# Differential attention: score matmuls of the two maps taken in turn from the two halves of TensorE's rows

## The reference, cut to what matters

```
s = jnp.einsum("bhiqd,bhikd->bhiqk", q, k).astype(jnp.float32) * scale   # i = 0, 1: two maps, d = 64
p = jax.nn.softmax(sc, axis=-1)
a = (p[:, :, 0] - lam_full * p[:, :, 1]).astype(v.dtype)
return jnp.einsum("bhqk,bhkd->bhqd", a, v)
```

## Time and profile before

| | us |
|---|---|
| median of 3 runs | 5064.48 |
| lowest, highest | 5056.97, 5072.84 |
| span of the profiled execution | 5071.2 |
| layer 1's attention in it, from the first score matmul to the last output copy | 925.3 |
| TensorE busy in the span | 4675.7 |

### The profile page before, as it was taken

How to read it: one execution, slowest core, us unless ns; L and a number is a source line. 1 busy time by engine, 2 the same in 40 slices (tenths; PEclk the granted TensorE clock), 3 DMA queues, 4 the chain that set the end, 5 groups by cost and what they waited for, 6 DMA issues and landing times. The chain is left out here.

```text
span 5071.2 us, 72044 instructions
## 1 busy us (share of the span) xinstructions
PE 4675.7 (92%) x29100; PEld 3834.2 (76%) x29100; DVE 1472.4 (29%) x2638; ACT 1065.5 (21%) x2197; POOL 558.0 (11%) x551
## 2 busy tenths in 40 slices
PE   7799999999689999999958999999895999999995
PEld 2377777774479999999955666666655999999995
DVE  6533344442311111111145444444422111111113
ACT  4333333331001111111122333333210111111112
POOL 0210000002310000000032000000032000000002
PEclk9899999999789999999979999999997999999997
DMA  8650010010356676776640000000106777777774
GB/s 310 202 193 20 20 39 20 20 42 30 130 174 238 236 241 236 240 241 233 236 139 31 13 13 12 12 12 12 47 33 223 256 246 255 253 252 251 255 255 150
DMA packets 563237, 737.79 MB, mean 145 GB/s; under 512 B 33680, under 2 KB 420352, under 8 KB 563032
## 3 DMA queue, kind: packets, MB, share of 16 engines
q1 hardware_dynamic: 533112, 642.58, 37.7%
q0 software_dynamic: 22352, 67.94, 3.7%
q10 hardware_dynamic: 7704, 26.31, 1.3%
HBM read 675.65 MB, written 65.05 MB: 146 GB/s over the span
## 5 line engine op out<-in xcount | busy, mean ns | idle before, releaser
L1444 PE MATMUL ps<-item_xT,expert_ring 128*128 128x160 f32 (+1 forms) x10496 | 1369.5, 293 | 6.8 <-issue 2.4
L1444 PEld LDWEIGHTS ps<-item_xT,expert_ring 128*128 128x128 f32 x10496 | 1360.4, 191 | 18.0 <-issue 18.0
L1466 PE MATMUL ps<-item_aT,expert_ring 128*128 128x144 f32 (+1 forms) x5248 | 763.6, 302 | 0.0
L1466 PEld LDWEIGHTS ps<-item_aT,expert_ring 128*128 128x128 f32 x5248 | 724.2, 198 | 5.5
L277 PE MATMUL ps<-hT,w_group 128*128 128x512 f32 (+1 forms) x1408 | 535.2, 539 | 6.0 <-ACT df_probs L1077 3.9
L1505 DVE TENSOR_TENSOR item_aT<-item_silu,ps 128x144 f32<-128x144 f32 (+1 forms) x328 | 102.4, 312 | 1249.4 <-ACT item_silu L1480 1249.4
L277 PEld LDWEIGHTS ps<-hT,w_group 128*128 128x128 f32 x1408 | 266.9, 192 | 257.1 <-issue 244.8
L1480 ACT ACTIVATE item_silu<-ps 128x144 f32<-128x144 f32 (+1 forms) x328 | 97.3, 297 | 1158.1 <-PE ps L1444 1158.1
L385 PE MATMUL ps<-hT,oT 128*128 128x512 f32 x576 | 254.2, 602 | 16.8 <-DMA router_w<-in_router_w 16.8
L1512 DVE COPY item_y<-ps 16x512 f32<-16x512 f32 (+1 forms) x82 | 55.7, 679 | 736.3 <-PE ps L1457 736.3
L1483 ACT ACTIVATE item_yT<-ps 128x144 f32<-128x144 f32 (+1 forms) x328 | 97.2, 296 | 811.7 <-PE ps L1466 811.7
(11 more groups left out here) (186 smaller groups left out, 4626.9 us busy)
## 6 DMA issues: line engine op xcount, KB each, us to landing
expert_ring<-in_expert_w_gate SPq DMA_DIRECT2D x164, 1024.0 KB, 5.0
expert_ring<-in_expert_w_up SPq DMA_DIRECT2D x164, 1024.0 KB, 7.2
expert_ring<-in_expert_w_down SPq DMA_DIRECT2D x82, 2048.0 KB, 10.0
mod_ring<-in_mod_w SPq DMA_DIRECT2D x24, 2048.0 KB, 11.1
w_group<-in_w_qkv SPq DMA_DIRECT2D x48, 512.0 KB, 4.8
slot_out<-item_y ACTq DMA_DIRECT2D x41, 512.0 KB, 7.1
slot_out<-rows POOLq DMA_DIRECT2D x5, 4096.0 KB, 36.4
h_rows<-hr SPq DMA_DIRECT2D x18, 512.0 KB, 2.6
```

The source lines that it names most:

```text
L1444: m = nc.tensor.matmul(gub(b, w), ring[:, b // 2, k, w * 256 + (b % 2) * P:w * 256 + (b % 2 + 1) * P], xT[:, k, :], start=k == 0, stop=k = ...
L1466: m = nc.tensor.matmul(yb(j), ring[:, 4 + j // 4, f, (j % 4) * P:(j % 4 + 1) * P], aT[:, f, :], start=f == 0, stop=f == FB - 1)
```

## The change

The two functions for scores become one. It waits for both exponentials of the previous tile before its first matmul, and its matmuls go in the order map 0 columns 1024 to 1279, map 1 columns 256 to 767 (in its own count), map 0 columns 0 to 511, then after the wait on `s_half` map 1's 256 columns, map 0 columns 512 to 1023, and map 1's last 512. The first increment of `s_S` comes with the fifth matmul, the second with the sixth. Matmuls, their sizes, their banks and all other engines' streams stay as they are.

```diff
-                        def scores(t, m, which):
+                        def score(t, m, n):
                             r = slice(m * HD, (m + 1) * HD)
-                            for n in which:
-                                c0, k0, w = parts[m][n]
-                                mm = nc.tensor.matmul(ps[:, c0:c0 + w], qT[r, t * P:(t + 1) * P], kT[r, k0:k0 + w], start=True, stop=True)
-                            return mm
-
-                        def scores_first(t):
+                            c0, k0, w = parts[m][n]
+                            return nc.tensor.matmul(ps[:, c0:c0 + w], qT[r, t * P:(t + 1) * P], kT[r, k0:k0 + w], start=True, stop=True)
+
+                        def scores(t):
                             if t:
 
-                                pe.wait_ge(s_exp, g * 2 * LT + 2 * t - 1)
-                            scores(t, 0, (0,))
-
-                        def scores_rest(t):
-                            if t:
-
                                 pe.wait_ge(s_exp, g * 2 * LT + 2 * t)
-                            scores(t, 0, (2,)).then_inc(s_half, 1)
-                            scores(t, 0, (1,))
+                            score(t, 0, 2).then_inc(s_half, 1)
+                            score(t, 1, 1)
+                            score(t, 0, 0)
 
                             pe.wait_ge(s_half, g * LT + t + 1)
-                            scores(t, 1, (0,)).then_inc(s_S, 1)
-                            scores(t, 1, (1, 2)).then_inc(s_S, 1)
+                            score(t, 1, 0)
+                            score(t, 0, 1).then_inc(s_S, 1)
+                            score(t, 1, 2).then_inc(s_S, 1)
...
-                        scores_first(0)
-                        scores_rest(0)
+                        scores(0)
...
-                        scores_first(1)
-                        scores_rest(1)
+                        scores(1)
...
-                                scores_first(t + 2)
-                                scores_rest(t + 2)
+                                scores(t + 2)
```

## The result

The changed kernel takes 5089.42 us (median of 9 runs, 5082.37 to 5108.4) against 5064.48 us (9 runs, 5051.89 to 5079.66). The ratio is 1.006, 95% interval 1.0041 to 1.0078: slower by about 30 us by the ratio and by 25 between the medians, where 13 us less were forecast. The profiled execution took 5108.4 us, with a span of 5106.4. It is the slowest of the nine, so the profile shows more of the loss than the median holds. The granted clock over its span was 0.944, the lowest of the nine (up to 0.949), and 0.954 in the profiled execution before.

What follows compares the result with a forecast made beforehand. TensorE was taken to bound each group's start, the VectorE and ScalarE loop tiles 2 to 7. Terms -1.41, -0.02, -0.20, -0.03 and 0 gave -1.66 per group, -13.3 us for 8 groups: 5064.5 to 5051.2, range 5036 to 5074.

Steps and rivals of the forecast that it cites:

- The ring: Tiles 2 to 7: combine, normalise, maxima and exponentials on VectorE and ScalarE set the 8.43 us period, without a TensorE wait.
- Rival 3: All tiles: TensorE bounds every one, so 90 us go and the time is 4974; chance 0.03.
- The lanes: Score passes: two row halves stream side by side; scores to next load take 2.54 us, not 3.95, 1.41 less per tile.
- rivals 1 and 2: Score passes: first, starts follow program order, end 2.98, +2 us, chance 0.10; second, long matmuls do not overlap, +74 us, 0.08.
- The sum at the start of a group: Tiles 0 and 1: earlier scores and V projection, shorter maxima and exponential wait; -1.66 us per group.
- Nothing gained, nothing lost: Tiles 2 to 7: VectorE is free 2.46 us after the load, map 0 ready at 2.45, so no change.
- rival 4: Clock: half-clock stretches in layer 1's experts may fall otherwise, up to 35 us; no fall expected in attention; chance 0.09.
- the sign, a clock under 1.00 in the stage: Attention stage of the changed profile: a granted clock below full would mean rival 4.
- theory B: Put for the experiments, on the scores: using both halves of the rows at once brings TensorE's clock down.
- theory C: Put for the experiments, on the scores: the later wait does the harm by itself, whatever the order; +25 us or more.
- The margin of 0.01 us: Tiles 2 to 7: slack between map 0 ready and VectorE free; each 0.1 us later costs 4.8 us there.
- The head start given up: Tiles 2 to 7: 0.56 us of TensorE score work ahead of the exponential is lost, paid for by the 1.41 saved.

Runs made afterwards that it cites:

- the split maximum: Alternating kernel without the full wait, VectorE's normalise behind the next maxima, plus map 1's maximum taken in two parts, bank 2 first; 4999.26 us, ratio 0.9857.
- the small filler's run: Changed kernel plus one unread 128-column matmul per tile between the second and third products with V; 5057.26 us, ratio 0.9971.
- the start-only run: Kernel before, with the new order and wait in tiles 0 and 1 of each group alone; 5055.84 us, ratio 0.9975.
- the last version: The split maximum's kernel, with tile 0 of each group given the changed kernel's full alternation; 4995.09 us, ratio 0.9845 against the kernel before.

## Why the prediction was wrong

- **The ring as bound of tiles 2 to 7: right.** Tiles at full clock kept 8.43 with scores 1.6 us shorter; cutting 0.43 out of VectorE's part of the ring gave 8.01, and the split maximum up to 7.27. Rival 3, TensorE as bound, is out.
- **The lanes: right in kind, the term too large.** The scores with what follows take 2.35 (3107.47 to 3109.82, below), not 2.54. I let the second half's first weights wait for two loads of the first half. In the trace the first loads of the two halves start 6 ns apart. Two 512-wide passes do run together at full rate: rivals 1 and 2 are out. The Trainium skill (TensorE: Matmul & The Clock Gate, Part 3) states that matmuls start in program order, by which rival 1 came to 2.98; the 2.35 of the trace doesn't agree.

TensorE after, group 3, tile 0, which answers to the earlier trace rows:

```profile
3107.47 2.42 PE L957 MATMUL ps<-df_kT,df_qT 64*128 64x256 f32 x12
3109.82 0.38 PE L937 MATMUL ps<-w_group,hT 128*128 128x128 f32 x1
```

- **The sum at the start of a group: right, mis-sized.** -1.87 per group where -1.66 was put, by the shorter scores. Where the clock holds, the gain comes out: the small filler's run and the start-only run are 15 and 13 us faster than before.
- **"Nothing gained, nothing lost" in tiles 2 to 7, the failed step.** It stood on rival 4's sentence "I expect no fall there, as products or scores fill most of each ring". I had counted the idle time, 1.2 to 1.7 us in 8.43, and judged it harmless without a price, because the whole stage had shown a clock of 1.00. That row was taken with a nearly full TensorE and said nothing of the new state. The clock fell 30 times, 29 of them under scores, and each fall cost 1.66 us: +49.7 against -15.0. The prediction had named the sign, a clock under 1.00 in the stage. That less work on TensorE ahead of the scores brings the fall was shown by adding work to the change and by taking work from the old order; theory B was refuted by the alternation without the full wait, theory C by the wait without the alternation. What counts as work, beyond busy time, stays open.
- **The margin of 0.01 us** was named, and it is what made a fall so dear: scores at half clock come 1.7 us late on a ring with no slack for them. The head start given up, 0.56 us ahead of the exponential, would have taken up a part of that; no run measures this by itself.
- **The chances.** Slower had 0.11, most of it for a mechanism that did not occur. The clock had 0.09, split evenly over the three outcomes, though in the changed stage it could only go down.

The Trainium skill (TensorE: Matmul & The Clock Gate, Part 1: The HAM clock gate) describes a gate that lets through half the clock when TensorE has lately done too little. The trace agrees in kind: 1.67 of 3.42 us busy, then half clock. Its section on a second failure mode (psum-queue depth-cycling) names short idle stretches between groups of matmuls, again and again, as enough to make the clock swing; 30 falls at gaps of 1.1 to 1.2 and 0.5 to 0.6 us agree. I had the gaps computed and did not set that section against them.

## What to carry to other kernels

When work on TensorE gets shorter while another ring sets the pace, the time saved becomes idle time; look at where it falls, and what runs next, before calling the edit free. If the next work is what the ring waits for, a fall of the clock can cost more than the edit gains (here 49.7 us against 15.0), and a little work in the gap, even useless work, can pay: here two passes of 0.11 us a tile turned +30 us into -15. A clock of 1.00 in the profile before is a statement about the load before. And if a ring sets the pace, cut the ring: the last version is 79 us faster than the kernel before, and the alternation at its best gave about 15.

## What the runs showed of the hardware

- Matmuls that contract over 64 partitions run on both halves of the rows at once at full rate, in float32: twelve passes with the next kind's load took 2.35 us in place of 3.95, and passes of 512 columns ran beside passes of 512.
- Idle stretches of 1.1 to 1.2 us and of 0.5 to 0.6, with 0.7 to 0.8 us of work between, were followed by half clock in 30 tiles and by full clock in others with the same rows; two passes of 0.11 us in the first gap were enough to end it.
- Passes on one half of the rows, busy for 2.51 of 3.40 us, were followed by half clock too, where 2.04 of 3.40 us in the small filler's kernel, most of it with passes on all 128 rows, were not.
